# Column order 16p+k, and 17 u tiles turned whole by VectorE, in a decoder layer with product-key experts

## What is computed

```python
h = rms(x, attn_norm_g);  proj = h @ w_in            # x: 512 tokens x 2048
x = x + concat(diff_attention(q, k, v), short_conv(B, C, xc)) @ w_out
h = rms(x, ffn_norm_g)
q  = (h @ w_q).reshape(t, 8, 2, 128)                 # 8 heads, two halves
sc = einsum("thcd,hckd->thck", q, subkeys)           # 128 keys for each half
top 16 of each half -> 256 sums -> top 16 -> experts (of 16384), gates = softmax(top)
act = gelu(sum_d u[experts] * h) * gates             # u, v: 16384 x 2048, float32
x = x + sum_k act_k * v[experts_k]
```

## Time and profile before

| | us |
|---|---|
| median of 3 runs | 2936.15 (2933.95 to 2936.56) |
| profiled execution, span | 2934.0 |
| TensorE busy in it | 2876.8 |
| VectorE busy | 2391.9 |
| ScalarE busy | 1056.2 |
| GpSimd busy | 1661.5 |

### The profile page before, as it was taken

The page is one execution under the profiler, slowest core; times in us unless marked ns, Lnnn a source line. Parts: engine busy times, 40 slices in busy tenths (PEclk is TensorE's granted clock), DMA queues, the critical chain, the costliest instruction groups (busy, mean ns, idle before and its releaser), DMA issues.

```text
span 2934.0 us, 40429 instructions
## 1 busy us (share of the span) xinstructions
PE 2876.8 (98%) x14769; PEld 2544.0 (87%) x14769; DVE 2391.9 (82%) x3106; ACT 1056.2 (36%) x1375; POOL 1661.5 (57%) x1078
## 2 busy tenths in 40 slices
PE   8999999999999999999999999999999999999999
PEld 6888778778899999999999999999997777877787
DVE  6555888855679898988889898899777998999898
ACT  4121333441334343434433343434233333333333
POOL 1000555500116677665766566577858888888772
PEclk9999999999999999999999999999999999999999
DMA  8998999979978999999999999999999999999999
GB/s 297 336 351 275 303 301 300 305 277 335 307 261 301 326 349 313 346 322 345 325 319 348 313 338 328 335 345 364 327 371 389 415 418 417 417 421 419 419 417 374
DMA packets 332718, 1010.00 MB, mean 344 GB/s; under 512 B 65748, under 2 KB 182496, under 8 KB 247072
## 3 DMA queue, kind: packets, MB, share of 16 engines
q1 hardware_dynamic: 181648, 523.28, 48.0%
q0 software_dynamic: 113344, 454.44, 42.7%
q10 hardware_dynamic: 37584, 30.43, 3.2%
HBM read 881.01 MB, written 127.01 MB: 344 GB/s over the span
## 4 chain that ended last, share of the span: by engine, by line
PE 59%; DVE 14%; POOL 9%; issue 8%; DMA 8%; ACT 1%; ACTq 0%; DVEq 0%; POOLq 0%; SPq 0%
PE ps L2011 19%; PE ps L2013 18%; PE ps L2012 18%; POOL dots L975 4%; DMA v_ring<-in_peer_v,experts 3%; DVE x_rows L1861 3%; POOL v_ring L986 2%; DMA v_two<-in_peer_v 2%; PE ps L2252 2%; POOL grid L967 2%; DVE x_one L1959 2%; DVE u_row L1852 1%; DVE uT_lo L1820 1%; DVE v_lo L1910 1%; DMA v_row<-in_peer_v,experts 1%
## 5 line engine op out<-in xcount | busy, mean ns | idle before, releaser
L2011 PE MATMUL ps<-hT_hi,uT_hi 128*128 128x384 f32 x2048 | 697.6, 341 | 6.2 <-DVE uT_lo L1820 2.6
L2013 PE MATMUL ps<-h2T_lo,uT_hi 128*128 128x384 f32 x2048 | 686.0, 335 | 0.0
L2012 PE MATMUL ps<-hT_hi,uT_lo 128*128 128x384 f32 x2048 | 684.9, 334 | 0.0
L967 POOL DMA_INDIRECT grid<-gates,grid_cells x256 | 544.6, 2127 | 79.9 <-issue 79.9
L2011 PE MATMUL ps<-v_hi,a_hi 128*128 128x512 f32 x1024 | 406.5, 397 | 26.5 <-DVE v_lo L1910 25.5
L2012 PE MATMUL ps<-v_hi,a_lo 128*128 128x512 f32 x1024 | 403.7, 394 | 0.0
L2013 PE MATMUL ps<-v_lo,a_hi 128*128 128x512 f32 x1024 | 403.4, 394 | 0.0
L1332 ACT ACTIVATE v_hi<-v_two 128x2048 fp32r<-128x2048 f32 x126 | 241.7, 1919 | 445.7 <-PE ps L2013 383.9
L2011 PEld LDWEIGHTS ps<-hT_hi,uT_hi 128*128 128x128 f32 x2048 | 384.6, 188 | 17.6 <-DVE uT_lo L1825 8.6
L2012 PEld LDWEIGHTS ps<-hT_hi,uT_lo 128*128 128x128 f32 x2048 | 384.9, 188 | 1.9
L2013 PEld LDWEIGHTS ps<-h2T_lo,uT_hi 128*128 128x128 f32 x2048 | 384.3, 188 | 0.0
(11 more groups left out here) (210 smaller groups left out, 4958.3 us busy)
## 6 DMA issues: line engine op xcount, KB each, us to landing
v_two<-in_peer_v SPq DMA_DIRECT2D x63, 2048.0 KB, 11.6
u_tile<-uT_all SPq DMA_DIRECT2D x70, 1024.0 KB, 6.7
u_tile<-in_peer_u SPq DMA_DIRECT2D x58, 1024.0 KB, 6.0
grid_rows<-grid SPq DMA_DIRECT2D x32, 1024.0 KB, 15.1
half_rows<-in_peer_u SPq DMA_DIRECT2D x58, 512.0 KB, 6.8
uT_all<-half_turned POOLq DMA_DIRECT2D x232, 128.0 KB, 5.0
near_rows<-in_peer_u SPq DMA_DIRECT2D x25, 1024.0 KB, 8.5
uT_all<-near_turned SPq DMA_DIRECT2D x100, 256.0 KB, 6.9
```

Of the source, the lines that this page charges most:

```text
L967: pool.indirect_dma_start(out=grid, out_offset=bass.IndirectOffsetOnAxis(ap=grid_cells[:, d, col:col + 1], axis=0), in_=gates[:, 2 + d, co ...
L2011: mm(out, a_hi, b_hi, start=first, stop=False)
L2012: mm(out, a_lo, b_hi, start=False, stop=False)
L2013: return mm(out, a_hi, b_lo, start=False, stop=last)
```

## The change

From the second norm on, depth index d = 16p + k stands at partition p of block k. So the query weights are loaded as `(p k) n`, TensorE's transposes of the normed rows and of u tiles read columns with a step of 16 elements (64 bytes), and VectorE's transposes for `uT_all` read with that step too and write contiguously.

In this order a quarter of a u tile's columns (512) belongs to a quarter of the partitions. 17 tiles are now **spread**: b = 6 and 10 of heads 0 to 5, b = 3, 5, 7, 9, 11 of the last. Four DMAs of 32 partitions put the four column quarters of such a tile into the four partition quarters of `u_tile`; VectorE turns it with four transposes of 32x32 blocks (128x512 each) straight into `ps_uT`, at the start of the iteration before; TensorE has no part in it. The extra tiles that are loaded turned move from b = 6 to b = 4. TensorE turns 41 tiles.

```diff
-EXTRA_AT = (6, 14)
+EXTRA_AT = (4, 14)
+SPREAD_AT = (6, 10)
+SPREAD_IN_LAST = (3, 5, 7, 9, 11)
+SPREAD = [TOPK * i + b for i in range(PEER_HEADS - 2) for b in SPREAD_AT]\
+    + [TOPK * (PEER_HEADS - 1) + b for b in SPREAD_IN_LAST]
...
-        w_q_v = peer_w_q[0].rearrange("(k p) n -> p k n", p=P)
+        w_q_v = peer_w_q[0].rearrange("(p k) n -> p k n", p=P)
...
+        spread_rows = [u_tile[b][:, :].rearrange("p (a d k) -> p k a d", a=QUADS, d=QUAD) for b in range(2)]
...
+                    elif last >= 0 and spread(last):
+                        sp.wait_ge(spread_turned, 4 * spread_until(last))
...
+                    if spread(tile):
+                        rows = u_table[tile * P:(tile + 1) * P, :].rearrange("(a e) (r m) -> r e a m", a=QUADS, r=QUADS)
+                        for r in range(QUADS):
+                            sp.dma_start(u_tile[b % 2][QUAD * r:QUAD * (r + 1), :].rearrange("e (a m) -> e a m", a=QUADS),
+                                         rows[r]).then_inc(u_tile_in[b % 2], 16)
...
-                rows = uT_all[bass.ds(row * P, P), :].rearrange("(r d) (a h m) -> a h d r m", r=QUADS, a=QUADS, h=HALVES)
+                rows = uT_all[bass.ds(row * P, P), :].rearrange("(h r d) (a m) -> a h d r m", h=HALVES, d=QUAD, a=QUADS)
...
+                if spread(tile):
+                    act.wait_ge(spread_turned, 4 * spread_until(tile) - 2 + 2 * half)
...
-                    v.transpose(seg_turned[pair][:, :, 4 * q:4 * q + 4, :].rearrange("p r k e -> p k r e"),
-                                seg_rows[pair][:, q * CHUNK:(q + 1) * CHUNK]
-                                .rearrange("p (k r d) -> p k r d", r=QUADS, d=QUAD))\
+                    v.transpose(seg_turned[pair][:, q, :, :],
+                                seg_rows[pair][:, q * CHUNK:(q + 1) * CHUNK].rearrange("p (d k) -> p k d", d=QUAD))\
...
+            def turn_spread(c):
+                dve.wait_ge(u_tile_in[c % 2], 16 * u_loads(c))
+                for q in range(4):
+                    v.transpose(ps_uT[q // 2][:, 4 * (q % 2):4 * (q % 2) + 4, :].rearrange("p k (a e) -> p k a e", a=QUADS),
+                                spread_rows[c % 2][:, 4 * q:4 * q + 4, :, :]).then_inc(spread_turned, 1)
...
+                    if spread(c + 1):
+                        turn_spread(c + 1)
                     if split_first:
                         split_u(c + 1, 0)
...
+                        rows = h_rows[:, t, k * P:(k + 1) * P] if n == 0 else\
+                            h_rows[:, t, :].rearrange("p (m k) -> p k m", m=P)[:, k, :]
...
+                rows = u_tile[buffer][:, :].rearrange("p (m k) -> p k m", m=P)
                 for k in range(8):
-                    last = turn(ps_uT[half][:, k, :], u_tile[buffer][:, (8 * half + k) * P:(8 * half + k + 1) * P],
-                                ident[:, :])
+                    last = turn(ps_uT[half][:, k, :], rows[:, 8 * half + k, :], ident[:, :])
...
-                        if more and not turned_before(c + 1):
+                        if more and not turned_before(c + 1) and not spread(c + 1):
```

More of the change, by code:

```diff
@@ L129, in turned_before, with spread, spread_until, u_loads @@
     return tile % 2 == 1 and tile < 2 * ODD_TURNED
+SPREAD_AT = (6, 10)
+SPREAD_IN_LAST = (3, 5, 7, 9, 11)
+SPREAD = [TOPK * i + b for i in range(PEER_HEADS - 2) for b in SPREAD_AT]\
+    + [TOPK * (PEER_HEADS - 1) + b for b in SPREAD_IN_LAST]
+def spread(tile):
+    return tile in SPREAD
+def spread_until(tile):
+    return sum(n <= tile for n in SPREAD)
+def u_loads(tile):
+    return sum(QUADS if spread(n) else 1 for n in range(tile % 2, tile + 1, 2))
 def kept_row(tile):
@@ L161, in turned_by_pe @@
 def turned_by_pe(parity, end):
-    return sum(tile % 2 == parity and not turned_before(tile) for tile in range(end))
+    return sum(tile % 2 == parity and not turned_before(tile) and not spread(tile) for tile in range(end))
 class Steps:
@@ L308, in decoder_layer @@
         half_rows.append(at("half_rows2", 124, [P, D // HALVES]))
-        half_turned = [nc.alloc_sbuf_tensor_at(f"half_turned{i}", [P, QUADS, KT // HALVES, QUAD], F32,
+        half_turned = [nc.alloc_sbuf_tensor_at(f"half_turned{i}", [P, QUADS // HALVES, KT, QUAD], F32,
                                                offset=late + 8 * KB + 4 * KB * i) for i in range(2)]
-        half_turned.append(at("half_turned2", 140, [P, QUADS, KT // HALVES, QUAD]))
+        half_turned.append(at("half_turned2", 140, [P, QUADS // HALVES, KT, QUAD]))
         wo0_hi = nc.alloc_sbuf_tensor_at("wo0_hi", [P, QUARTER, CHUNK], F32R, offset=late)
@@ L1263, in split_u @@
                     if half == 0:
-                        act.wait_ge(u_tile_in[tile % 2], 16 * (tile // 2 + 1))
+                        act.wait_ge(u_tile_in[tile % 2], 16 * u_loads(tile))
                     nc.scalar.activation(uT_hi[half][:, :, :].rearrange("p k (a e) -> p k a e", a=QUADS),
@@ L1267, in split_u @@
                     return
-                if half == 1:
+                if spread(tile):
+                    act.wait_ge(spread_turned, 4 * spread_until(tile) - 2 + 2 * half)
+                elif half == 1:
                     act.wait_ge(uT_half1_ps[b % 2], turned_by_pe(b % 2, tile + 1))
@@ L1465, in turn_half @@
                 for q in range(2):
-                    v.transpose(half_turned[x][:, :, 4 * q:4 * q + 4, :].rearrange("p r k e -> p k r e"),
-                                half_rows[x][:, q * CHUNK:(q + 1) * CHUNK]
-                                .rearrange("p (k r d) -> p k r d", r=QUADS, d=QUAD))\
+                    v.transpose(half_turned[x][:, q, :, :],
+                                half_rows[x][:, q * CHUNK:(q + 1) * CHUNK].rearrange("p (d k) -> p k d", d=QUAD))\
                         .then_inc(seg_ready[NEAR], 1)
@@ L2004, in turn_rows @@
                     for k in range(4 * b, 4 * b + 4):
-                        last = turn(turned_bank(n, t, b)[:, (k % 4) * P:(k % 4 + 1) * P],
-                                    h_rows[:, t, k * P:(k + 1) * P], ident[:, :])
+                        rows = h_rows[:, t, k * P:(k + 1) * P] if n == 0 else\
+                            h_rows[:, t, :].rearrange("p (m k) -> p k m", m=P)[:, k, :]
+                        last = turn(turned_bank(n, t, b)[:, (k % 4) * P:(k % 4 + 1) * P], rows, ident[:, :])
                 last.then_inc(hT_ps, 1)
@@ L2246, in _, with turned @@
                 first_queries(slice(2 * P, SEQ), quarter, 4 * (2 * TB - 1) + quarter + 1, last=quarter == 3)
-            def turned(buffer, use, half):
+            def turned(buffer, loads, half):
                 if half == 0:
-                    pe.wait_ge(u_tile_in[buffer], 16 * use)
+                    pe.wait_ge(u_tile_in[buffer], 16 * loads)
+                rows = u_tile[buffer][:, :].rearrange("p (m k) -> p k m", m=P)
                 for k in range(8):
-                    last = turn(ps_uT[half][:, k, :], u_tile[buffer][:, (8 * half + k) * P:(8 * half + k + 1) * P],
-                                ident[:, :])
+                    last = turn(ps_uT[half][:, k, :], rows[:, 8 * half + k, :], ident[:, :])
                 last.then_inc(uT_half0_ps if half == 0 else uT_half1_ps[buffer], 1)
@@ L2271, in sweep @@
                             summed.then_inc(swept[b % 2], 1)
-                        if more and not turned_before(c + 1):
-                            turned(nxt, TOPK // 2 * i + (b + 1) // 2 + 1, half)
+                        if more and not turned_before(c + 1) and not spread(c + 1):
+                            turned(nxt, u_loads(c + 1), half)
                         elif more and half == 0:
```

9 lines of the change are left out of this document (6 added, 3 removed).

## The result

| | before | after |
|---|---|---|
| median of the runs | 2935.05 us (2933.92 to 2936.56, 4 runs) | 2986.77 us (2980.88 to 2991.15, 4 runs) |
| profiled execution, span | 2934.0 | 2983.1 |

The ratio is 1.0173, with a 95% interval of 1.0161 to 1.0185: **52 us slower**, and the forecast was 9 us faster, 2927. The range ended at 2965.

The account below looks back on a forecast made before the run. TensorE was taken to set the sweep's pace. Of 30.3 us removed, losses at tile 4 (10.7), tile 10 (4.5 to 6.2) and the last head (5.0) left 8.4 to 10.1, taken as 9: 2927 us, range 2916 to 2965.

Parts of the forecast that it names:

- The order of columns: Reads with a 64-byte step on TensorE and VectorE: counted as nothing; upper bound for a VectorE transpose 1.22 us for 0.67.
- case D: Rival: the stepped read slows VectorE's transposes by 0.54 us each, in the sweep and attention heads; 2968 us, chance 0.13.
- The term for the heads: Attention heads, within case D: 8.6 us more on 42.9 busy of 50, 1.5 over; some 10 us in seven heads.
- Case C: Rival: the stepped weight read lengthens TensorE's 720 transposes by 0.11 us each; 2986 us, 2955 at 47 ns; chance 0.15.
- slower: 0.30: The chance given to the changed kernel being slower; about 6 us was what can be told from no change.
- Price of a turn, 1.78 us: One tile's 16 transposes on TensorE in the sweep take 1.78 us, covered by nothing; 17 tiles removed make 30.3 us.
- Tile 4 gives nothing: Each head's sweep: VectorE is already late with tile 4's second half, so TensorE waits the 1.78 us; 10.7 us lost.
- Tile 6 costs nothing: Each head's sweep: tile 6's spread transposes on VectorE delay both halves, but both still fit; no cost.
- Tile 10 keeps 1.0: Heads 0 to 5: 0.75 of 1.78 us lost to waits, 1.0 kept; counted as 4.5 to 6.2 us over 6 heads.
- Last head keeps 3.9: Five spread tiles: waits of 0.55 us at four and 2.8 at the first; 5.0 of 8.9 us lost, 3.9 kept.
- The loads are covered: Four DMAs per spread tile cost 1.0 us more on SP; tile 6's load has 12.4 us, longest landing 12.7: covered.
- TensorE's idle time in the sweep rises by 20 us, at these places: Sign of being right: about 20 us more waiting for `uT_lo`, at tile 4's and 10's second halves and last head's odd tiles.

Follow-up runs that it names:

- e3: The changed kernel with whole runs instead of the 64-byte step in TensorE's 720 transposes only: 2980.97 us.
- e1: The changed kernel with whole runs instead of the 64-byte step in every read, on VectorE and TensorE: 2939.19 us.
- s1: The changed kernel with steps of 8, 16 and 32 bytes in VectorE's early transposes, 8 and 16 in TensorE's of u tiles: 2980.4 us (one run).
- r2: The changed kernel with a column order whose step is two elements (8 bytes) and no tile spread: 2947.75 us.
- e4: The changed kernel with whole runs instead of the 64-byte step in the 68 spread transposes only: 2965.42 us.
- f2: The changed kernel with its column order kept but no tile spread, TensorE turning 58 tiles: 2965.29 us.
- g1: e1 (no step, 17 spread tiles) with one plain DMA of 128 rows for each spread tile instead of four: 2934.46 us.
- g3: g1 with only ten tiles spread, tile 10 of heads 0 to 5 and tiles 5, 7, 9, 11 of the last: 2930.02 us.

## Why the prediction was wrong

**The failed step** is "The order of columns": "I take nothing for both". For TensorE that was nearly right (e3 gives back 5.8 us), for VectorE wrong. The argument was that VectorE takes as long for one operand as for two and so isn't at the end of what it reads. The row that it needed was one with a step, and there was none. The upper bound given beside it, "1.22 us for 0.67", held: it is 1.04. Two rows on other operations were no reason to choose the lower end, and the 0.13 for case D was too little. With the step taken out everywhere (e1, on TensorE too), 47.6 of the 52 us are back. The Trainium skill (Advanced Engine Details and Errata, SBUF Cachelines) says that a read which meets a new 16-byte line each time is penalised and that two hits on a line absorb the latency. For VectorE the run with steps (s1) agrees: 0.68 us at 8 bytes, 1.06 at 16. For TensorE's weight load it doesn't: 8 bytes already cost (209 ns for 141 in r2).

**Case D had the mechanism, and another sum than the runs.** It gave 2968: ten us in the heads and 31 in the sweep, for 0.54 us more a transpose. Measured were 0.37 us more a transpose, 25 us before the sweep and 35 in it (25.6 more than before where 9 less were forecast). In the sweep the step is not all of it: whole runs in the spread transposes alone make it 24 us shorter (e4, 1319.9 for 1343.7), and without any step it still is 17 us above the forecast (e1). The term for the heads was made as a balance: 8.6 us more on 42.9 of 50 busy. By that balance the real price (16 x 0.37 = 5.9 us) would have fitted into the idle time, and nothing would have been lost. It isn't idle time that pays: TensorE waits for `probs` eight times, and the heads lost 13 us. And the q, k, v stage, in which VectorE turns u tiles too, wasn't in the sum at all: 9.2 us.

**Case C** had the right number for the wrong reason. The weight load got 53 ns longer, near the 47 that the prediction bounded, but the spacing hardly changed: eight transposes in front of the next matmul, before and after:

```profile
2052.23 1.03 PE L2252 MATMUL ps<-ident,u_tile 128*128 128x128 f32 x8
2053.02 0.42 PE L2011 MATMUL ps<-hT_hi,uT_hi 128*128 128x384 f32 x1
```

```profile
2109.27 1.06 PE L2295 MATMUL ps<-ident,u_tile 128*128 128x128 f32 x8
2110.08 0.42 PE L2053 MATMUL ps<-hT_hi,uT_hi 128*128 128x384 f32 x1
```

0.79 and 0.81 us. 12.5 ns a transpose were given as the point from which C decides; it is 3 to 5 (f2). The 2955 us that C names for 47 ns isn't worked out there: its terms put that between 2940 (30.3 us saved in full) and 2961 (34 on top of the forecast). And "slower: 0.30" is more than C and D have together, 0.28.

**Point by point:**

- *Price of a turn, 1.78 us.* Its half is right: -0.88 in an interval in which VectorE wasn't late (g1, g3). No tile gave both halves, since VectorE was late for the other one each time.
- *Tile 4 gives nothing.* Right, in all heads and also without a step: -0.9, then +0.9.
- *Tile 6 costs nothing.* Right without a step (0.0 in g1's third head); with it 0.5 a head (forecast by D: 1.2).
- *Tile 10 keeps 1.0.* Right without a step from the third to the sixth head (-0.9 to -1.0), wrong in the second (+0.2 in g1, +0.7 in g3); with the step +0.5 in the third, so each spread tile's 1.5 us (3.92 for 2.40) came out in full.
- *Last head keeps 3.9.* For tiles 5 to 11 right: in g1 TensorE waits four times 0.52 or 0.53 us (at 2077.23, 2096.45, 2115.68 and 2134.91) for an odd tile's `uT_lo`, where 0.55 was computed, and each gives 1.0 (forecast 1.2). For tile 3 the wait is right (2.73 in g1, 2.74 in e1, forecast 2.8). Its cost was to be 1.0: it is 1.3 in e1, where the granted clock held, and 2.6 in g1, where it fell (below).
- *The loads are covered.* Wrong. I reckoned with the landing times of the earlier trace rows, 12.7 us at the longest, as if four DMAs were as good as one and nothing else was on its way. With four DMAs and the later release together the load behind took 18.5 us (e1). Without a step the four DMAs cost 4.7 us (e1 against g1); in the changed kernel itself, in which VectorE is later than the loads, most of it is covered (ScalarE waits 10.8 us for `uT_all` in all).
- *TensorE's idle time in the sweep rises by 20 us, at these places.* The places are right; the amount was 38 (1390 - 1344.4 against 1340 - 1332).
- *9 us kept.* Not even without the step: e1 is 12 us off that. With four DMAs replaced by one and without tiles 3, 4 and 6, it is 6.3.

## What to carry to other kernels

A read pattern that an operation of the trace has never had needs a price of its own from a small kernel, or the upper bound goes into the sum, above all where it changes operations elsewhere in the program that nobody meant to touch. More work on a helper engine isn't paid out of its idle share: look for who waits behind it, operation by operation. When a buffer is freed later than before and its load is cut into smaller DMAs, look at what else is on the DMA queues at the new time: here either alone did little, and both together made a load land after 18.5 us.
